# Two decoder layers on one core: gathers read the residual rows with scaled selections, and half a gate matrix is loaded into the space of the scaled rows

## What is computed

```python
def hier_moe(h, ...):                  # h is rms_norm(h, ffn_norm[layer])
    grp = top_k(softmax(x2 @ w_group + b_group), 1)
    top_v, top_i = top_k(fine logits inside grp, 2)
    gates = g_val * softmax(top_v)
    ...
    # per expert e, on the tokens that chose it:
    hid = silu(xb @ w_gate[e]) * (xb @ w_up[e])
    out[tokens] += gate * (hid @ w_down[e])
```

## Time and profile before

| | before |
|---|---|
| median of 3 runs | 1111.41 us (1110.23 to 1111.61) |
| profiled execution | span 1110.1 us, 21758 instructions; the page gives no other time of it |
| busy, share of the span | PE 76%, PEld 48%, DVE 34%, ACT 22%, POOL 3% |
| DMA | 440.73 MB, mean 397 GB/s |

### The profile page before, as it was taken

How to read it: one execution, slowest core, us unless ns; L and a number is a source line. 1 busy time by engine, 2 the same in 40 slices (tenths; PEclk the granted TensorE clock), 3 DMA queues, 4 the chain that set the end, 5 groups by cost and what they waited for, 6 DMA issues and landing times.

```text
span 1110.1 us, 21758 instructions
## 1 busy us (share of the span) xinstructions
PE 847.7 (76%) x9146; PEld 537.9 (48%) x9146; DVE 380.6 (34%) x926; ACT 243.8 (22%) x622; POOL 37.6 (3%) x63
## 2 busy tenths in 40 slices
PE   9999979856576767576799999797666656676775
PEld 6877735524243434343488776454333324343432
DVE  6888323312121212021288663323211112121212
ACT  5566301100000000000165763111010000000012
POOL 0013100000000000000000211000000000000000
PEclk9999989978887868788999999899787878888888
DMA  9898899999999999999999668999999999999996
GB/s 353 262 389 329 344 401 425 430 428 430 428 427 430 428 428 430 427 427 430 409 386 363 226 268 337 423 426 428 429 428 429 429 428 429 428 429 430 427 427 256
DMA packets 56577, 440.73 MB, mean 397 GB/s; under 512 B 12113, under 2 KB 12625, under 8 KB 31058
## 3 DMA queue, kind: packets, MB, share of 16 engines
q1 hardware_dynamic: 56240, 440.02, 95.5%
q10 hardware_dynamic: 290, 0.07, 0.0%
HBM read 439.03 MB, written 1.05 MB: 396 GB/s over the span
## 4 chain that ended last, share of the span: by engine, by line
DMA 42%; PE 40%; SPq 10%; another core or an unknown queue 3%; DVE 2%; ACT 2%; issue 1%; ACTq 0%; DVEq 0%; POOL 0%; POOLq 0%
DMA ring<-in_w_expert_up 25%; DMA ring<-in_w_expert_down 15%; PE banks L1120 11%; PE banks L1148 4%; PE banks L999 4%; SPq L520 3%; PE banks L1003 3%; PE banks L1000 3%; SPq L468 3%; PE banks L1161 2%; SPq L472 2%; PE banks L1090 2%; PE banks L1216 1%; PE banks L1218 1%; PE banks L1217 1%
## 5 line engine op out<-in xcount | busy, mean ns | idle before, releaser
L1120 PE MATMUL banks<-ring,scratch 128*32 128x256 f32 x4096 | 297.4, 455 | 174.0 <-DMA ring<-in_w_expert_up 173.5
L1120 PEld LDWEIGHTS banks<-ring,scratch 128*32 128x32 f32 x4096 | 152.9, 130 | 313.0 <-issue 175.1
L1632 DVE TENSOR_SCALAR scratch<-scratch 128x128 f32<-128x128 f32 x64 | 14.6, 228 | 618.4 <-ACT scratch L763 605.2
L762 ACT ACTIVATE scratch<-banks 128x128 f32<-128x128 f32 x64 | 17.8, 278 | 573.5 <-PE banks L1120 554.8
L1148 PE MATMUL banks<-ring,h 128*32 128x256 f32 x2048 | 128.0, 390 | 12.8 <-DMA ring<-in_w_expert_down 12.6
L1161 PE MATMUL banks<-h 32*128 32x256 f32 x1024 | 74.4, 403 | 36.5 <-ACT h L772 36.5
L1148 PEld LDWEIGHTS banks<-ring,h 128*32 128x32 f32 x2048 | 62.9, 111 | 58.8 <-issue 25.0
L1161 PEld LDWEIGHTS banks<-h 32*128 32x128 f32 x1024 | 50.2, 187 | 65.8 <-issue 65.8
L999 PE MATMUL banks<-split,h_high 128*128 128x512 f32 x192 | 77.6, 404 | 0.6 <-DVE split L1424 0.2
L1424 DVE SCALAR_TENSOR_TENSOR split<-ring,gains,split 128x512 fp32r<-128x512 f32 x96 | 69.8, 766 | 23.2 <-ACT split L810 22.6
L1003 PE MATMUL banks<-split,h_low 128*128 128x512 f32 x192 | 75.2, 391 | 0.0
(11 more groups left out here) (173 smaller groups left out, 739.0 us busy)
## 6 DMA issues: line engine op xcount, KB each, us to landing
ring<-in_w_expert_gate SPq DMA_DIRECT2D x62, 2048.0 KB, 47.5
ring<-in_w_expert_up SPq DMA_DIRECT2D x61, 2048.0 KB, 48.9
ring<-in_w_expert_down SPq DMA_DIRECT2D x56, 2048.0 KB, 49.2
ring<-in_w_in_even SPq DMA_DIRECT2D x5, 2048.0 KB, 18.1
ring<-in_w_expert_down SPq DMA_DIRECT2D x10, 1024.0 KB, 10.1
ring<-in_w_in_odd SPq DMA_DIRECT2D x5, 2048.0 KB, 19.7
ring<-in_w_expert_up SPq DMA_DIRECT2D x6, 1024.0 KB, 10.8
ring<-in_w_out_even SPq DMA_DIRECT2D x2, 2048.0 KB, 9.0
```

Of the source, the lines that this page charges most:

```text
L1120: last = pe.matmul(psum[6][32 * j:32 * j + 32, 0:2 * P].rearrange("p (a s) -> p a s", a=2), xT[:, c, SLOTS * k:SLOTS * k + SLOTS], ring[:, ...
```

## The change

- No scaled rows are made: ACT's L925 is gone. `gather_first` and `gather` read h through `h_c`. The scale goes into the selections: `first_choice` is four instructions for each t (compare, then multiply with `rstd`), `choose_slots` a second one for each later group.
- `gated`, `gatedT`, `hidT` and `y_sb` lie over `xn` in place of `h`, which stays whole to the end of the layer. `sums_begun` is gone. `gate_slots` makes its own 0/1 selection and so is two instructions.
- As soon as `load_first` is issued, SP loads the first half of expert 4's gate matrix (128 x 2048, 1 MiB) into `xn`, named `stage`, without waiting for `piece_used`. POOL (768 of its 2048 columns) and DVE (1280) copy it into the ring, after expert 0's first half is used, and before DVE's first `hidden`. After `piece_used` SP loads only the first half of up.
- The second half of the turned h for t = 1 goes into `scratch` in place of `xn`, and ACT's copy waits for the logits of t = 0.
- DVE's `gate_slots` for experts 0 and 1 stand between and behind their `hidden`, not both after.

```diff
+                sp.dma_start(stage, gate_rows[row][:, 0:512 * FIRST_PIECES[0]]).then_inc(stage_arrived, 16)
                 for i, end in enumerate(FIRST_PIECES):
...
                     for n, rows in enumerate((gate_rows, up_rows)):
-                        sp.dma_start(ring[:, PAIR_AT[0] + n, cols], rows[row][:, cols]).then_inc(pair_arrived[l][0], 16)
+                        if i or n:
+                            sp.dma_start(ring[:, PAIR_AT[0] + n, cols], rows[row][:, cols])\
+                              .then_inc(pair_arrived[l][0], 16)
...
+            def copy_stage(l):
+
+                pool.wait_ge(piece_used, (len(FIRST_PIECES) - 1) * l + 1)
+                pool.wait_ge(stage_arrived, 16 * (l + 1))
+                pool.tensor_tensor(ring[:, PAIR_AT[0], 0:STAGE_POOL], stage[:, 0:STAGE_POOL],
+                                   const("ones")[:, 0:1].broadcast_to([P, STAGE_POOL]), ALU.mult).then_inc(stage_copied, 1)
...
-                        act.activation(xn_c[:, t, c, :], h_c[:, t, c, :], ACT.Copy,
-                                       scale=rstd[:, t:t + 1]).then_inc(xn_scaled, 1)
...
-                    last = pe.matmul(psum[4 + c // 4][:, P * (c % 4):P * (c % 4) + P], xn_c[:, t, c, :],
+                    last = pe.matmul(psum[4 + c // 4][:, P * (c % 4):P * (c % 4) + P], h_c[:, t, c, :],
                                      onehot[:, t, :, :].rearrange("p k s -> p (k s)"),
...
-                dve.tensor_tensor(onehot[:, t, :, :], const("slots").unsqueeze(1).broadcast_to([P, GE, SLOTS]),
-                                  place_bank[t][:, 0:GE].unsqueeze(2).broadcast_to([P, GE, SLOTS]),
-                                  ALU.is_equal).then_inc(onehot_ready[l], 1)
+                for k in range(GE):
+                    last = dve.tensor_scalar(onehot[:, t, k, :], const("slots"), place_bank[t][:, k:k + 1],
+                                             rstd[:, t:t + 1], ALU.is_equal, ALU.mult)
+                last.then_inc(onehot_ready[l], 1)
...
+            def copy_stage(l):
+
+                dve.wait_ge(stage_arrived, 16 * (l + 1))
+                dve.tensor_copy(ring[:, PAIR_AT[0], STAGE_POOL:2048], stage[:, STAGE_POOL:2048])\
+                   .then_inc(stage_copied, 1)
+                dve.wait_ge(stage_copied, STAGE_COPIES * (l + 1))
...
-                dve.wait_ge(sums_begun, l + 1)
+                dve.wait_ge(gate_steps, GATE_STEPS * (l + 1))
+                copy_stage(l)
                 for k in range(AHEAD):
-                    hidden(l, k, k, first=(k == 0))
-                dve.wait_ge(gate_steps, GATE_STEPS * (l + 1))
-                dve.wait_ge(onehot_ready[l], T)
-                for k in range(AHEAD):
-                    gate_slots(l, k, k)
+                    hidden(l, k, k, first=(k == 0), links=0)
+                    gate_slots(l, k, k, k, links=SILU_LINKS)
```

More of the change, by code:

```diff
@@ L91 @@
 FIRST_PIECES = (4, 8)
-EXTRA_LOADS = [{0: 2 * len(FIRST_PIECES) - 2, GE - 1: l} for l in range(LAYERS)]
+EXTRA_LOADS = [{0: 2 * len(FIRST_PIECES) - 3, GE - 1: l} for l in range(LAYERS)]
 EXTRA_DOWNS = {2: 1, 3: 1}
@@ L198 @@
 SILU_LINKS = 3
+EXPERT_LINKS = SILU_LINKS + 1
+STAGE_COPIES = 2
+STAGE_POOL = 768
 def build(nc, x, mix_even, w_in_even, w_out_even, mix_odd, w_in_odd, w_out_odd, ffn_norm,
@@ L295, in build @@
         xT = scratch[:, 0:1024].rearrange("p (c s) -> p c s", c=C)
[L296 removed]
+        hT_late = [v.rearrange("p (c s) -> p c s", c=C // 2) for v in (scratch[:, 1024:1536], scratch[:, 0:512])]
         def hT(t, q):
@@ L304, in build @@
         hid = scratch[:, 1664:1792]
[L305 to L309, removed]
+        stage = xn[:, 0:2048]
+        gated = [xn[:, 256 * i:256 + 256 * i].rearrange("p (t b s) -> p t b s", t=T, b=4) for i in range(GE)]
+        gatedT = xn[:, 1024:1280]
+        hidT = [xn[:, 1280 + 128 * i:1408 + 128 * i] for i in range(GE)]
+        y_sb = xn[:, 1792:2048]
         acc_half = [banks[:, 2 * i:2 * i + 2, :].rearrange("p q (t n) -> p t q n", t=T) for i in range(2)]
@@ L903, in turned_out @@
                     act.wait_ge(h_turned, 4 * (2 * l + 1) + 2 * q + t + 1)
+                    if t and q:
+                        act.wait_ge(logits_done, T * l + 1)
                     act.copy(hT(t, q),
@@ L1099, in gather_first @@
                 for c in range(C):
-                    if c % 4 == 0:
-                        pe.wait_ge(xn_scaled, 2 * (T * l + t) + c // 4 + 1)
-                    last = pe.matmul(psum[4 + c // 4][:, P * (c % 4):P * (c % 4) + P], xn_c[:, t, c, :],
+                    last = pe.matmul(psum[4 + c // 4][:, P * (c % 4):P * (c % 4) + P], h_c[:, t, c, :],
                                      onehot[:, t, :, :].rearrange("p k s -> p (k s)"),
@@ L1114, in gate_up @@
                 if k == 0:
+                    if not first:
+                        pe.wait_ge(stage_copied, STAGE_COPIES * (l + 1))
                     pe.wait_ge(xT_ready[l], group_no(r, g) * 2 + 1)
@@ L1165, in start_sums @@
             def start_sums(q):
-                last = pe.matmul(acc[q], ident, h[:, :, QUARTER * q:QUARTER * q + QUARTER], start=True, stop=False)
-                if q == 3:
-                    last.then_inc(sums_begun, 1)
+                pe.matmul(acc[q], ident, h[:, :, QUARTER * q:QUARTER * q + QUARTER], start=True, stop=False)
             def spread_gains(half):
@@ L1623, in columns, with hidden @@
                                       ALU.mult).then_inc(xT_ready[l], 1)
-            def hidden(l, e, k, first=False):
-                chain = Chain(dve, dve_moe[l], e * SILU_LINKS)
+            def hidden(l, e, k, first=False, links=1):
+                chain = Chain(dve, dve_moe[l], e * EXPERT_LINKS + links)
                 dve.wait_ge(gate_up_out[l], e + 1)
@@ L1646, in group @@
                     if k < GE - AHEAD:
-                        gate_slots(l, ahead, GE * g + ahead)
+                        gate_slots(l, ahead, GE * g + ahead, e + AHEAD)
                     elif after:
-                        gate_slots(l, ahead, GE * after[1] + ahead)
+                        gate_slots(l, ahead, GE * after[1] + ahead, e + AHEAD)
                     if k == GE - AHEAD - 1 and after:
```

27 lines of the change are left out of this document (17 added, 10 removed).

## The result

| | before | after |
|---|---|---|
| median | 1111.31 us (4 runs, 1110.23 to 1111.61) | 1119.56 us (4 runs, 1118.82 to 1120.33) |
| ratio | | 1.0069, 95% interval 1.0057 to 1.0082 |
| profiled execution, span | 1110.1 us | 1118.3 us |
| PE busy | 76% | 81% |

The changed kernel is slower by 0.69%: 7.7 us by that ratio; the medians stand 8.25 us apart, the spans 8.2. The forecast was 1107.3 us, with 1113.6 as its upper end. In the changed kernel `gather_first` is L1104, `gather` L1094, `gate_up` L1124, SP's pieces L605 (stage) and L614, `first_choice` L1578, `columns` L1638.

What follows compares the result with a forecast made beforehand. Expert stages were taken as bound by DMA bytes at about 428 GB/s plus idle holes. Staged half -4.9, delay +2.4, second hole -1.6 make -4.1 us: span 1110.1 to 1106.0, median 1.3 above, so 1107.3 us; range 1105.0 to 1113.6.

Steps and rivals of the forecast that it cites:

- I choose this reading: Gather's weight loads from h, 8 elements apart: strided columns come one in 0.91 ns, so 6 ns more a load, 0.2 us a layer.
- the factor: Gather's weight loads: strided reads take twice the time of contiguous ones, 110 ns becoming 220 for the columns; 27% chance.
- the delay of `piece_used`: Head of each layer: SP's wait for expert 0's first half ends 1.2 us later, +2.4 us in all.
- The first rival: Gathers at each layer's head: strided loads take twice as long, `piece_used` 4.3 us later, twice; 1113.5 us; 27% chance.
- The staged half: First DMA hole of each layer: 1 MiB issued early uses 2.45 us of it, -4.9 us in all.
- The selections: DVE at each layer's head: four instructions for one cost 0.5 us more each, 1.0 us a layer (0 to 1.3).
- The second hole: DMA rate dip at 159 to 162 us, layer 0 alone: closes because `hidden` begins earlier, -1.6 us; staying open, 7%.
- What costs nothing: ACT's L925 going brings nothing; second selection instructions, ACT's added wait and later gathers' loads are covered, adding nothing.
- The guess of 0.5: PE after L1167, layer 0: some 0.5 us of standstill remains for reading the number of rounds.

## Why the prediction was wrong

**The step that failed** is "I choose this reading: 0.05 x 128 = 6 ns a load". The strided transposes had shown a column in 0.91 ns, and I took this as a rate at which columns are delivered to any load. An ordinary load took 334 - 191 = 143 ns more, not 6. Less the 81 ns taken as fixed, its columns took 253 ns, 1.98 each, where a transpose's take 0.91 by the same step: the rate of one kind of load was not that of the other. Why the two kinds differ, no run shows. The nearer forecast was the factor, which transposes and ACT's copies had both shown.

In the sum, the delay of `piece_used` was set at 1.2 us a layer and measured 6.0 and 6.3. Of layer 0's 6.0, the two selections are 2 x (0.94 - 0.29) = 1.3, the two gathers 2 x 2.13 = 4.3, and the slow start of the product 0.7. These add up to 6.3; 0.2 go off because the first selection began at 125.35 and not at 125.57. The first rival, with 4.3, had the mechanism and the place right and was too small by the larger factor (253 to 110 ns, not 2), and by the clock, which no case had.

**The staged half, -4.9 us:** the transfer went as said. What I missed is the dip behind the wait, which gives some 1.0 us a layer back. Only 1 MiB is issued at the end of the wait where there were two, but that this makes the dip isn't shown. So the forecast would not have held with the loads priced right either: side by side the change came to 0.9991, some 1 us, not 4.1. The dip is up to 2 us of that gap; the rest stays open.

**The selections:** 0.65 each in place of 0.5, at the upper bound.

**The second hole, -1.6 us:** closed as said. PE's standstill was 2.91 us, not under 2. The profile puts its end down to DVE's L1622, but the one for expert 0, for which PE waits, was over at 145.55, and the standstill began at 148.27. With the gathers side by side the same gap is 2.53 us and named `issue`: PE waits there for nothing that the profile shows, and in its program it loads the number of rounds and enters the loop. The guess of 0.5 for that was some 2 us too small. It was short enough.

**What costs nothing:** held. The second instructions of the later selections and the later gathers' loads are covered; the run with only the head side by side has both and is at 0.999.

With these sizes the sum is -4.9 + 12.3 + 2.1 - 1.6 = +7.9 us; the spans differ by 8.2. The rest, 0.3, I haven't placed.

## What to carry to other kernels

A price belongs to a kind of instruction: a rate read from transposes did not hold of an ordinary weight load of the same step, and where two other kinds had both doubled, doubling was the nearer forecast. Where a kernel waits for transfers, the same slow instruction was free in the stream and cost its full length at the head, so change the layout only where it is covered. Before a layout is changed to make one read contiguous, look at what it does to the runs of the transfers.

## What the runs showed of the hardware

- An fp32 weight load of 128x128 takes 191, 196, 328 and 334 ns for steps of 1, 2, 4 and 8 elements, where a transpose's takes 140 at 1 and 197 at 8; a gather of 16 with the step of 8 takes 4.05 us at a granted clock of 1.00 and 4.18 at 0.60.
- The granted clock was 0.60 in the first gather of the changed kernel, in which PE counted as busy 4.16 of 4.20 us, and the product behind the gathers began at 0.51. In the kernel before, read 8 apart, it was 1.00 in the first gather, 0.78 in the second and 0.50 at the start of the product. With loads side by side it stayed at 1.00.
- With gate and up in runs of 16, 8, 4 and 2 KB (the down matrices unchanged) the weights arrived at 429, 424, 416 and 400 GB/s.
- Between `start_sums` and the first instruction of its loop PE stood still for 2.53 us without waiting for anything that the profile shows, in the kernel with the gathers side by side.
